# A two-block network in one kernel: head norm moved into the attention rounds, early output projection, and re-ordered seams

## The reference, cut to what matters

```python
def diff_attend(q, k, v, lam):
    s = jnp.einsum('bqhcd,bkhcd->bhcqk', q, k) * ATTN_SCALE
    p = jax.nn.softmax(s, axis=-1)
    a = p[:, :, 0] - lam * p[:, :, 1]
    return jnp.einsum('bhqk,bkhe->bqhe', a, v)

def merge_heads(o, f, subln_g, fourier_w, w_out, lambda_init):
    o = (rmsnorm(o, subln_g) * (1.0 - lambda_init)).reshape(B, T, DIFF_WIDTH)   # norm of each head
    return jnp.concatenate([o, fourier_groups(f, fourier_w)], axis=-1) @ w_out
...
# first_block, layer 0: attention + Fourier mixer; layer 1: conformer convolution
x = x + mod_l[2] * y_l
x = x + mod_l[5] * swiglu(modulate(rmsnorm(x, ffn_norm_g[i]), mod_l[3], mod_l[4]), w1, w3, w2)
...
# second_block: an RG-LRU layer (projection, causal convolution, gates, scan), then attention
```

## Time and profile before

| | us |
|---|---|
| median of 3 executions | 989.19 |
| profiled execution, its own time | 991.08 |
| its span | 989.4 |
| PE busy | 915.5 (93%) |
| DVE busy | 740.9 (75%) |
| ACT busy | 467.8 (47%) |
| POOL busy | 136.1 (14%) |

### The profile page before, as it was taken

One profiled execution on the slowest core, in us unless ns is written; L12 is line 12 of the kernel. 1 busy time (PEld: TensorE's weight loads), 2 busy tenths in 40 slices (PEclk: granted clock), 3 DMA queues, 4 the chain that ended last, 5 costly groups with the idle time before them and its releaser, 6 DMA issues.

```text
span 989.4 us, 12483 instructions
## 1 busy us (share of the span) xinstructions
PE 915.5 (93%) x4323; PEld 718.3 (73%) x4323; DVE 740.9 (75%) x1074; ACT 467.8 (47%) x777; POOL 136.1 (14%) x204
## 2 busy tenths in 40 slices
PE   3799999899999999899978999999978998999995
PEld 0588766677888888677656688888867786777884
DVE  0598787788777768669687787677687788877574
ACT  1542247555434443453166443444336775645661
POOL 0001120404100121031001500020001020011000
PEclk8799999899999999989999999999999999999999
DMA  9987662358998888637533698898865546595001
GB/s 352 374 299 256 237 235 88 123 170 268 382 339 279 311 318 300 210 133 255 192 129 127 210 359 310 285 339 300 288 217 192 164 156 201 203 364 202 31 22 42
DMA packets 119046, 229.09 MB, mean 232 GB/s; under 512 B 8650, under 2 KB 64684, under 8 KB 119002
## 3 DMA queue, kind: packets, MB, share of 16 engines
q1 hardware_dynamic: 92608, 141.57, 41.5%
q0 software_dynamic: 24224, 86.32, 25.2%
q10 hardware_dynamic: 2170, 0.64, 0.3%
HBM read 227.43 MB, written 1.08 MB: 231 GB/s over the span
## 4 chain that ended last, share of the span: by engine, by line
PE 75%; DVE 13%; ACT 5%; issue 4%; DMA 2%; POOL 1%; SPq 0%; ACTq 0%; POOLq 0%; DVEq 0%
PE bank L1952 21%; PE bank L1954 20%; PE bank L1953 20%; DVE w_lo L1208 2%; DMA w_land<-ev_w_in_dram 2%; PE bank L2484 1%; DVE x L1290 1%; DVE w_lo L1321 1%; DVE tmp L1289 1%; PE bank L2325 1%; PE bank L2174 1%; PE bank L2032 1%; ACT w_hi L675 1%; DVE xT_lo L1334 1%; DMA ident<-k_ident_dram 1%
## 5 line engine op out<-in xcount | busy, mean ns | idle before, releaser
L1952 PE MATMUL bank<-w_hi,xT_hi 128*128 128x512 f32 x800 | 324.4, 406 | 21.1 <-DVE xT_lo L1334 10.3
L1954 PE MATMUL bank<-w_hi,xT_lo 128*128 128x512 f32 x800 | 314.8, 394 | 0.0
L1953 PE MATMUL bank<-w_lo,xT_hi 128*128 128x512 f32 x800 | 314.7, 393 | 0.0
L1208 DVE TENSOR_TENSOR w_lo<-w_land,w_hi 128x2048 fp32r<-128x2048 f32 x110 | 251.9, 2295 | 74.0 <-ACT w_hi L675 73.7
L675 ACT ACTIVATE w_hi<-w_land 128x2048 fp32r<-128x2048 f32 x110 | 210.3, 1915 | 117.5 <-PE bank L1954 115.1
L1952 PEld LDWEIGHTS bank<-w_hi,xT_hi 128*128 128x128 f32 x800 | 152.2, 190 | 64.1 <-issue 22.7
L1954 PEld LDWEIGHTS bank<-w_hi,xT_lo 128*128 128x128 f32 x800 | 152.0, 190 | 33.0
L1953 PEld LDWEIGHTS bank<-w_lo,xT_hi 128*128 128x128 f32 x800 | 152.4, 191 | 28.9
L1225 DVE SCALAR_TENSOR_TENSOR job_sum<-a_land,silu_c,job_sum 128x1024 f32<-128x1024 f32 x126 | 163.4, 1297 | 10.0 <-DMA a_land<-mod_w_dram 4.6
L1952 PE MATMUL bank<-w_hi,hT_hi 128*128 128x512 f32 x176 | 69.9, 397 | 2.8 <-DVE hT_lo L1579 2.8
L1954 PE MATMUL bank<-w_hi,hT_lo 128*128 128x512 f32 x176 | 68.7, 390 | 0.0
(11 more groups left out here) (325 smaller groups left out, 1121.4 us busy)
## 6 DMA issues: line engine op xcount, KB each, us to landing
w_land<-ffn_w_dram SPq DMA_DIRECT2D x132, 512.0 KB, 5.7
a_land<-ada_w_dram POOLq DMA_DIRECT2D x40, 1024.0 KB, 6.0
a_land<-mod_w_dram POOLq DMA_DIRECT2D x24, 1024.0 KB, 5.6
w_land<-od_pw_w_dram SPq DMA_DIRECT2D x24, 512.0 KB, 4.9
w_land<-ev_w_in_dram SPq DMA_DIRECT2D x20, 512.0 KB, 11.8
w_land<-ada_w_dram SPq DMA_DIRECT2D x16, 512.0 KB, 11.3
a_land<-kv_mod_w_dram POOLq DMA_DIRECT2D x8, 1024.0 KB, 6.6
w_land<-rg_w_in_dram SPq DMA_DIRECT2D x16, 512.0 KB, 5.0
```

What stands on the lines that cost most here:

```text
L1208: dve.tensor_tensor(w_lo[u % N_SPLIT][:, :], w_land[n % N_LAND][:, :], w_hi[u % N_SPLIT][:, :].bitcast(F32), ALU.subtract).then_inc(s_lo, 1)
L1952: pe.matmul(dst, hi, whi, start=start, stop=False)
L1953: pe.matmul(dst, hi, wlo, start=False, stop=False)
L1954: return pe.matmul(dst, lo, whi, start=False, stop=stop)
```

## The change

No product and no element is added or left out. What changes is where things stand:

- Rounds. PE makes the first part of the token tiles' late values ahead of round 0, and the others one round later than their old counter says (rounds 1, 2, 3). ACT copies late values one tile at a time. On DVE the splits of units 10 and 11 move from rounds 0 and 3 to rounds 3 and 4.
- Head norm. Mean square of heads 0 to 3 in round 9 and their scaling in round 10; heads 4 and 5 after the rounds. POOL's two powers are 8 and 4 columns wide (before 10 and 2), and its load of `a_land` unit 2 of job 3, which stood before the powers, now stands behind both and behind the load of `gate`.
- Job 3. Its units 0 and 1, which DVE did in rounds 10 and 11, now stand between the steps of the output operand.
- Output projection. PE turns heads 0 to 3 in round 11, and `out_chunk` starts unit 10 on them for t=0, then the Fourier product, two k-slices of t=1, the turn of heads 4 and 5, and the rest.
- Ends of both feed-forward stages. The second half of a split, and in the second one two small modulation instructions, move behind the first residual steps; the third residual step moves ahead of `xn`.
- rg_in. PE turns chunk 0 after the first 12 products of chunk 1; ACT and DVE split one unit (base+4) ahead of the work on chunk 0.

```diff
 # POOL
-            load_job(3, ada[0], 5 * D, (2,))
-            pow_heads(1, 0, 10)
-            pow_heads(2, 10, 12)
+            pow_heads(1, 0, 8)
+            pow_heads(2, 8, 12)
             pool.wait_ge(sem("four_ft"), 2)
             load_gate("out", gate)
-            load_job(3, ada[0], 5 * D, (3,))
+            load_job(3, ada[0], 5 * D, range(2, 4))
 # ACT
-            act.wait_ge(sem("in_ctx"), 1)
+            late_value(1, 0, (sem("in_ctx"), 1))
+            act.wait_ge(sem("in_ctx"), 2)
             exps(0)
-            late_values(1)
+            late_value(1, 1, (sem("in_ctx"), 2))
...
+                else:
+                    spectrum_rows(0)
+                    spectrum_rows(1)
...
                 if n == 11:
-                    spectrum_rows(0)
+                    full_hi("sub", o_full, xT_hi, range(2))
                 if n >= 1:
                     head_out(n - 1)
...
+            full_hi("sub", o_full, xT_hi, range(2, 4), 2)
             head_out(len(ITS) - 1)
-            spectrum_rows(1)
-            full_hi("sub", o_full, xT_hi, range(HEADS))
+            full_hi("sub", o_full, xT_hi, range(4, HEADS), 4)
...
+            split_hi(base + 4)
             act.wait_ge(sem("ru_zero"), 1)
             rg_turned(0)
-            split_hi(base + 4)
 # DVE
-                if n == 0:
-                    split_lo(10)
-                if n == 3:
-                    split_lo(11)
+                if n in (3, 4):
+                    split_lo(n + 7)
-                if n >= 10:
-                    job_units(3, (n - 10,))
+                if n == 9:
+                    heads_mean(0, 4)
+                if n == 10:
+                    heads_normed(1, 0, 4)
...
-            heads_normed(1, 0, HEADS - 1)
-            heads_normed(2, HEADS - 1, HEADS)
-            full_lo("sub", o_full, ..., range(HEADS), 12)
+            job_units(3, (0,), None, (0,))
+            full_lo("sub", o_full, ..., range(4))
+            heads_mean(4, HEADS)
+            job_units(3, (0,), None, (1,))
+            heads_normed(2, 4, HEADS)
+            job_units(3, (1,))
+            full_lo("sub", o_full, ..., range(4, HEADS), first=4)
...
                 split_lo_half(ahead, 0, half_ready(ahead))
-                split_lo_half(ahead, 1, (s_hi, ahead + 1)).then_inc(s_lo, 1)
-                if layer == 1:
-                    mod_cols(...); link(...); dve.wait_ge(sem("final_sq"), 1)
                 residual(*steps[0])
                 residual(*steps[1])
+                if layer == 1:
+                    mod_cols(...); link(...); dve.wait_ge(sem("final_sq"), 1)
                 tile_mean(after, 0, 2)
+                residual(*steps[2])
                 tile_normed(after, 0)
-                residual(*steps[2])
+                split_lo_half(ahead, 1, (s_hi, ahead + 1)).then_inc(s_lo, 1)
...
             for c in range(2):
-                if c == 1:
+                split_lo(base + 2 * c + 3)
+                if c == 0:
                     split_lo(base + 4)
-                split_lo(base + 2 * c + 3)
 # PE
+            def turn_heads_out(heads):
+                if heads[0] == 0:
+                    pe.wait_ge(sem("d_exp"), 2 * len(ITS))
+                pe.wait_ge(*seen("xn", "sub", NT if heads[0] == 0 else 2 * NT))
+                for h in heads: ...   # two transposes each
...
+            pe.wait_ge(sem("in_act"), 7)
+            late_value_products(0, 0, (0,))
             for n in range(len(ITS)):
...
                 turn_diff(n)
+                if n == 11:
+                    turn_heads_out(range(4))
...
-                if n < 4:
+                if 1 <= n < 4:
                     late_value_products(0, n // 2, (n % 2,))
...
+            def out_chunk(u, banks):
+                pe.wait_ge(sem("four_fts"), 2)
+                unit_wait(u)
+                half(u, 0, xT_hi, xT_lo, banks, None, "sub", (0,))
+                ...   # Fourier product
+                half(u, 0, xT_hi, xT_lo, banks, None, None, (1,), (0, 1))
+                turn_heads_out(range(4, HEADS))
+                half(u, 0, xT_hi, xT_lo, banks, s_used, None, (1,), (2, 3))
+                unit_wait(u + 1)
+                half(u + 1, 1, xT_hi, xT_lo, banks, None, "sub", (0,), (0, 1))
+                pe.wait_ge(sem("four_lo"), 2)
+                half(u + 1, 1, xT_hi, xT_lo, banks, None, None, (0,), (2, 3), part=True)
+                half(u + 1, 1, xT_hi, xT_lo, banks, s_used, None, (1,))
...
+                        if (c, j, t) == (1, 0, 0):
+                            turn_pair("rg_in", rg_tok, rg_free)(0)
...
-                turn_pair("rg_in", rg_tok, rg_free)(c)
+                if c >= 1:
+                    turn_pair("rg_in", rg_tok, rg_free)(c)
```

More of the change, by code:

```diff
@@ L706, in half_squares, with full_hi @@
                                    accum_out=ss[:, 2 * t + c:2 * t + c + 1]).then_inc(sem("ss"), 1)
-            def full_hi(stage, full, hi, ks=range(KT)):
+            def full_hi(stage, full, hi, ks=range(KT), first=0):
                 for n, k in enumerate(ks):
-                    act.wait_ge(*seen("full", stage, n + 1))
+                    act.wait_ge(*seen("full", stage, first + n + 1))
                     act.activation(hi[:, k, :], full[:, k, :], ACT.Copy).then_inc(sem("hi"), 1)
@@ L878, in spectrum_rows, with late_value @@
                 act.activation(ftT[:, f, :], bank[f][:, :], ACT.Copy).then_inc(sem("four_fts"), 1)
[L880 to L886 removed]
+            def late_value(src, t, ready):
+                act.wait_ge(*ready)
+                act.activation(v_tok[:, (NT if src == 0 else 0) + t, 256:768], bank[6 + t][:, :], ACT.Copy).then_inc(sem("in_act"), 1)
+            late_value(1, 0, (sem("in_ctx"), 1))
+            act.wait_ge(sem("in_ctx"), 2)
             exps(0)
[L888 removed]
+            late_value(1, 1, (sem("in_ctx"), 2))
             for n in range(len(ITS)):
@@ L1256, in mod_cols, with full_lo @@
                 link(dve.scalar_tensor_tensor(out=a_col[:, :], in0=mc(v_scale), scalar=1.0, in1=g, op0=ALU.add, op1=ALU.mult))
-            def full_lo(stage, full, hi, lo, banks, a, b, ks=range(KT), turns=2 * KT, whole=False):
+            def full_lo(stage, full, hi, lo, banks, a, b, ks=range(KT), turns=2 * KT, whole=False, first=0):
                 if whole:
@@ L1263, in low @@
                 def low(n):
-                    dve.wait_ge(*seen("hi", stage, n + 1))
+                    dve.wait_ge(*seen("hi", stage, first + n + 1))
                     dve.tensor_tensor(lo[:, ks[n], :], full[:, ks[n], :], hi[:, ks[n], :].bitcast(F32),
@@ L1492, in _, with heads_mean, heads_normed @@
             row_max(0)
+            def heads_mean(h0, h1):
+                a, b = 2 * h0, 2 * h1
+                dve.wait_ge(*seen("ss", "sub", b))
+                dve.tensor_scalar(ms[:, a:b], ss[:, a:b], 1.0 / P, EPS, ALU.mult, ALU.add).then_inc(sem("ms"), 1)
+            def heads_normed(part, h0, h1):
+                dve.wait_ge(*seen("rstd", "sub", part))
+                r = rstd[:, 2 * h0:2 * h1].rearrange("p (h t) -> p t h", t=NT)
+                for t in range(NT):
+                    o = o_tok[:, t, h0 * P:h1 * P].rearrange("p (h e) -> p h e", e=P)
+                    dve.tensor_tensor(o, o, r[:, t, :].unsqueeze(2).broadcast_to([P, h1 - h0, P]), ALU.mult).then_inc(sem("xn"), 1)
             for n, (h, t) in enumerate(ITS):
@@ L2141, in _ @@
             ITS = [(h, t) for h in range(HEADS) for t in range(NT)]
+            def turn_heads_out(heads):
+                if heads[0] == 0:
+                    pe.wait_ge(sem("d_exp"), 2 * len(ITS))
+                pe.wait_ge(*seen("xn", "sub", NT if heads[0] == 0 else 2 * NT))
+                for h in heads:
+                    for t in range(NT):
+                        pe.transpose(bank[2 + h // 2][:, 256 * (h % 2) + t * P:256 * (h % 2) + t * P + P],
+                                     o_tok[:, t, h * P:h * P + P], ident[:, :]).then_inc(sem("tr"), 1)
             def scores(n):
@@ L2204, in _ @@
             turn_heads(3)
-            late_value_products(1, 1).then_inc(sem("in_ctx"), 1)
+            for t in range(NT):
+                late_value_products(1, 1, (t,)).then_inc(sem("in_ctx"), 1)
+            pe.wait_ge(sem("in_act"), 7)
+            late_value_products(0, 0, (0,))
             for n in range(len(ITS)):
@@ L2288, in dense @@
                         after(c)
-            dense("out", 2, "sub", mid=gate_mid("out"), norm_after="n_ffn0")
+            dense("out", 2, "sub", first=out_chunk, norm_after="n_ffn0")
             def ffn(layer, loops, first_job):
```

50 lines of the change are left out of this document (16 added, 34 removed).

## The result

The first set of executions gave 982.05 us for the changed kernel (median of 8 executions, 980.39 to 984.94) against 991.17 for the one before (8 executions, 987.23 to 992.52): ratio 0.9909, 95% interval 0.9885 to 0.9934. Two later sets, 6 and 9 executions against 29 and 14 of before, gave 983.38 against 989.77 (0.9943, 0.9921 to 0.9966) and 983.64 against 990.00 (0.9950, 0.9931 to 0.9970). Over everything timed, the medians are 983.5 (23 executions) and 990.0 (64). The gain is thus about 6.4 us; the 9.1 of the first set was partly luck.

What follows compares the result with a forecast made beforehand. The prediction took PE as the bound (75% of the chain of waits), with DVE feeding the output stage. Terms 1.0 + 3.1 + 0.3 + 0.8 + 1.2 = 6.4 us gave 982.8 us against the 989.19 median, range 979.2 to 987.3.

Steps and rivals of the forecast that it cites:

- A1: Rounds: late-value products fill PE's 1.54 us wait in round 0, DVE's chain runs earlier; 1.0 us (-0.1 to 1.5).
- A2: Head norm and output projection: PE's wait behind the rounds goes, but DVE sets the gain; 3.1 us (1.0 to 6.9).
- The four waits that were to leave: DVE, rounds' end to `xn`: net waits for POOL's two powers, for PE and for ACT go; 4.55 us.
- The rule that was weighed and set aside: Second power beside a two-input DVE instruction: SBUF contention could make `rstd` 1.0 us later, whole gain 5.5 instead of 6.5.
- The slow clock: Behind the rounds: idle PE costs twice, by its wait and by 6.8 us at about half clock behind it.
- B0: End of feed-forward 0: half split and third residual step reordered, PE starts earlier; 0.3 us (0 to 0.7).
- C: rg_in: 12 products of the next chunk fill PE's 1.18 us wait, later convolution stays covered; 1.2 us (0.4 to 1.3).
- B1: End of feed-forward 1: residual starts 1.1 earlier, `xn` 0.5, first product moves from 742.46 to 741.65; 0.8 us (0.3 to 1.2).
- R1: Rival: around PE's new waits the clock falls and takes back up to 3.4 us; 985.5 us, chance 0.13.
- R4: Rival: clock falls behind several new waits in output stage and round 1; 993 us with three falls, chance 0.05.
- R2: Rival: gains given back downstream by late a_land, slower power or rg_in's DVE chain, 2 to 3 us; 985.5, chance 0.14.
- R3: Rival: the slow stretch at 738.9 or at 418 is halved too, 3 us more; 980 us, chance 0.08.

Runs made afterwards that it cites:

- b_only: The kernel before with only the edits at the two feed-forward ends; 986.99 us, ratio 0.9983 (12 executions).
- c_only: The kernel before with only the edits of rg_in; 988.93 us, ratio 0.9989 (12 executions).
- before_fill: The kernel before plus four unread PE products behind the last product of the rounds, filling the 3.85 us wait; 988.94 us, ratio 0.9991.
- after_best: Changed kernel: job instructions moved to round 10 and ahead of the first o_full, ACT's unit 12 split ahead of its head 4 and 5 copies; 981.47 us, 0.9924.
- a_only: The kernel before with only the edits of rounds, head norm and output projection; 985.77 us, ratio 0.9962 (12 executions).
- a1_only: The kernel before with only 12 early late-value products, ACT's single copies and the two moved splits; one execution, second to last scores 48.26 us.

## Why the prediction was right, step by step

- **A1** was 1.0 and measured 0.8 (0.9 to 1.1 against b_only and c_only, whose low clock also stands near 123; 1.2 where neither has it, 47.92 us in before_fill against 46.68 and 46.67 in the two later profiles of the changed kernel). The filling products, the row maximum behind them and the cover for the split in round 4 are as told; the wait for round 1's `diff` is 1.16 (forecast 1.4). Alone it gave 0.5 to 0.8.
- **A2** was 3.1 and measured 2.8. On DVE, from the end of round 11's `diff` to `xn`, 32.1 us became 29.3. The four waits that were to leave left, 4.55. The new short waits are larger than told: 0.52, 0.32 and 0.91, less 0.69 that went (ahead of two `xT_lo`), so 1.06 instead of 0.75 (the pieces named in the prediction add up to 0.7). The wrong piece is the second power, estimated at 1.0 from its neighbours' widths and 1.99 in fact: right alone (1.02), wrong beside DVE. It cost a wait of 0.91 that the sum did not have; the 0.6 put down for upper parts and the late turn did not come, so the sum missed by only 0.3, by luck. A wait for the second power is also one of the prediction's own signs of being wrong. The rule that was weighed and set aside held (the Trainium skill, GPSIMD Engine Reference, section "Key points"); the 5.5 us that it made of the whole (5.4 by the sum of 6.4; the prediction writes 6.5 there) is 0.4 below the measured 5.9, the forecast's 6.4 is 0.5 above.
- **PE behind it.** Forecast 1.3 and 2.0 for `w_lo` and `xn`, 3.3 together; measured 0.86, 0.86 and 1.67, 3.4 together. One more wait than told, ahead of head 4's lower part, and the same sum, because DVE sets it. POOL's load of unit 2 was issued at 187.44 (forecast 187.7), and DVE never waited for it.
- **The slow clock** behind the rounds was rightly seen as a price of the wait (before_fill shows it). How long it is was not as fixed as the earlier trace rows made it look: 6.8 us in one execution of this code, 3.4 in three others, so A2 is worth 1.4 to 1.75 against those (40.03, 40.37 and 40.39) and 2.8 against the profile shown. Nor were the low stretches three: behind 100 us before has six, 3.4 us at 124, 6.8 at 186, 6.8 at 418, 3.4 at 438, 3.4 at 500 and 6.8 at 739.
- **What A2 is made of.** before_fill, which leaves the order of the work as it is, has 2.4 of the 2.8: DVE's waits for PE and ACT of 1.14, 0.54 and 0.49 go once the turns and the Fourier product run at full clock. The new order adds 0.4, since the powers' waits of 2.92 and the scaling of 1.3 leave, and two job instructions (2.0) and three new waits (1.75) come.
- **The agreement of 6.4 with 6.4** is partly luck. The distances give 5.9 with the 6.8 us stretch of the profile shown. With the 3.4 us stretch of the other executions they give 4.8, or 5.3 with the A1 of 1.2, and the remaining 1.1 to 1.6 us of the timed gain went with the clock at other places.
- **B0** 0.4 (0.3), **C** 1.4 (1.2, and above its upper bound of 1.3 by 0.1). C's cover held. The 0.25 us above the wait of 1.18 is no new effect: from the start of the last product to the start of the turn it was 1.56 us, 1.33 more than the 0.23 from one product to the next.
- **B1** was 0.8 and measured 0.45: the mis-sized term. `xn` came 0.36 earlier, not 0.5. At the first product the gain is 0.67, and 0.2 of it returns at the waits behind it, which I had not followed.
- **The rivals.** R1 and R4 did not happen: in none of the profiles with the whole change does the clock fall between 137 and 225 (after_best has 3.4 us of it from 228). R2's downstream losses are the 0.2 of B1. R3 happened in part: the low stretch at 418 to 425 stands in before and c_only (in before_fill 3.4 us of it), in none of the three profiles of the changed kernel, and that at 739 stays. I cannot call it the change's work: a_only, which leaves that seam as it was, lost it as well, and so did b_only and a1_only.

What stays open is which edit raises the mean clock over the span. It isn't the filled wait alone: before_fill removed that stretch and has the clock of before. The traces point at feed-forward 0. Between 405 and 460 the granted clock is 0.91 in before, before_fill and c_only, the three with the lowest mean clock of the kernels timed more than once, and 0.97 or 1.00 in the eleven other profiles, with the edits of the rounds or of the feed-forward ends. But this is one profile of most kernels, and why either edit does it is not shown.

## What to carry to other kernels

When PE waits for an engine that feeds the whole place, go through that engine's instructions one by one: filling PE's wait moves it behind the filling, and what arrives is what the feeding engine gains. Fill the wait with work for nobody first: here that alone gave 2.4 us of the 2.8 in the distance, through the clock, and in the time no gain that can be told from none. A duration read from a row where both VectorE and GpSimd are alone does not hold beside each other; ask who starts first and add the rest of the other's instruction. Where low-clock stretches wander from run to run, judge parts of 1 us by distances between marks in the traces, and the whole by many executions.
